# PEER sweep with gates in 2 KB rows, activations in pairs, and gathered slots at 32, 16 and 80

## The reference

```
q = (x @ w_q).reshape(T, 8, 2, 128); s = q . sub_keys      # 128 keys a side, 8 heads
top 16 per side, 16 best of the 256 sums per head -> idx (T, 128); g = softmax(best scores)
a = x . u_tab[idx];  wgt = g * gelu(a)
y = sum over the 128 chosen experts of wgt * v_tab[idx]
```

## Time and profile before

| what | value |
|---|---|
| median of 3 runs | 2556.61 us (2554.44 to 2559.3) |
| profiled execution | 2554.05 us, its span 2552.2 us |
| granted TensorE clock, mean | 0.962 of full speed |
| PE busy | 2294.7 us, 90% |
| DVE / ACT / POOL busy | 68% / 36% / 43% |
| moved by DMA | 771.11 MB, mean 302 GB/s |

### The profile page before, as it was taken

The page is one execution under the profiler, slowest core; times in us unless marked ns, Lnnn a source line. Parts: engine busy times, 40 slices in busy tenths (PEclk is TensorE's granted clock), DMA queues, the critical chain, the costliest instruction groups (busy, mean ns, idle before and its releaser), DMA issues.

```text
span 2552.2 us, 39867 instructions
## 1 busy us (share of the span) xinstructions
PE 2294.7 (90%) x11829; PEld 1696.5 (66%) x11829; DVE 1744.0 (68%) x3945; ACT 912.5 (36%) x1694; POOL 1109.0 (43%) x612
## 2 busy tenths in 40 slices
PE   6697999999877999999989689999998769999998
PEld 3676999999874333333368389989998754444443
DVE  7986798888554766666669856988886553444444
ACT  3254455666542111111044254656665420000001
POOL 2623587777782222222224035777777841111110
PEclk8898999999998999999999799999999989999999
DMA  7423378999999999999942023679999999999995
GB/s 298 157 78 128 110 228 300 383 387 383 403 418 393 387 394 394 394 394 394 378 155 92 0 83 109 185 269 376 383 377 392 420 378 368 369 384 385 374 381 206
DMA packets 284091, 771.11 MB, mean 302 GB/s; under 512 B 26080, under 2 KB 160352, under 8 KB 248544
## 3 DMA queue, kind: packets, MB, share of 16 engines
q1 hardware_dynamic: 169664, 401.76, 44.0%
q0 software_dynamic: 36864, 268.45, 25.9%
q10 hardware_dynamic: 77472, 99.78, 10.8%
HBM read 701.08 MB, written 68.81 MB: 302 GB/s over the span
## 4 chain that ended last, share of the span: by engine, by line
PE 56%; DMA 16%; issue 13%; DVE 8%; POOL 3%; SPq 2%; ACT 2%; ACTq 0%; DVEq 0%; POOLq 0%
PE ps L1718 26%; DMA raw<-in_v 7%; PE ps L1484 7%; PE ps L1485 7%; PE ps L1486 7%; PE ps L1700 4%; POOL w_lo L585 3%; DMA work<-in_uv,picked 2%; DMA hf<-in_uv,picked 2%; DMA hots<-in_uv,picked 1%; DMA uv_stat<-in_uv,picked 1%; SPq L554 1%; DVE ps L1364 1%; DVE ga L1030 1%; PE ps L1653 1%
## 5 line engine op out<-in xcount | busy, mean ns | idle before, releaser
L585 POOL TENSOR_TENSOR w_lo<-raw,w_hi 128x1024 fp32r<-128x1024 f32 x330 | 801.3, 2432 | 573.6 <-ACT w_hi L677 571.5
L1718 PE MATMUL ps<-raw,work 128*128 128x512 f32 x2048 | 906.0, 603 | 68.0 <-DMA raw<-in_v 41.5
L1484 PE MATMUL ps<-h_hi,w_hi 128*128 128x256 f32 (+1 forms) x2560 | 776.4, 303 | 75.2 <-POOL w_lo L585 74.9
L1718 PEld LDWEIGHTS ps<-raw,work 128*128 128x128 f32 x2048 | 392.2, 193 | 580.6 <-issue 576.2
L1485 PE MATMUL ps<-h_lo,w_hi 128*128 128x256 f32 (+1 forms) x2560 | 754.6, 295 | 0.0
L1486 PE MATMUL ps<-h_hi,w_lo 128*128 128x256 f32 (+1 forms) x2560 | 754.3, 295 | 0.0
L1484 PEld LDWEIGHTS ps<-h_hi,w_hi 128*128 128x128 f32 x2560 | 492.3, 192 | 92.6 <-POOL w_lo L585 91.7
L1485 PEld LDWEIGHTS ps<-h_lo,w_hi 128*128 128x128 f32 x2560 | 492.8, 193 | 0.0
L1486 PEld LDWEIGHTS ps<-h_hi,w_lo 128*128 128x128 f32 x2560 | 491.8, 192 | 0.0
L677 ACT ACTIVATE w_hi<-raw 128x1024 fp32r<-128x1024 f32 x330 | 347.7, 1056 | 118.1 <-DMA raw<-in_in 39.0
L1412 DVE TENSOR_TENSOR work<-work 128x256 f32<-128x256 f32 x256 | 106.3, 422 | 412.6 <-DMA work<-g_dram 340.6
(11 more groups left out here) (195 smaller groups left out, 2287.4 us busy)
## 6 DMA issues: line engine op xcount, KB each, us to landing
raw<-in_u SPq DMA_DIRECT2D x256, 512.0 KB, 6.9
raw<-in_v SPq DMA_DIRECT2D x256, 512.0 KB, 8.8
a_dram<-ga ACTq DMA_DIRECT2D x256, 128.0 KB, 7.8
work<-g_dram SPq DMA_DIRECT2D x64, 512.0 KB, 11.3
work<-a_dram ACTq DMA_DIRECT2D x248, 128.0 KB, 9.0
g_dram<-work ACTq DMA_DIRECT2D x16, 1920.0 KB, 11.5
work<-in_mod_w SPq DMA_DIRECT2D x56, 512.0 KB, 10.9
hots<-in_mod_w SPq DMA_DIRECT2D x32, 512.0 KB, 3.6
```

What stands on the lines that cost most here:

```text
L585: nc.gpsimd.tensor_tensor(w_lo[:, m % RING, :], raw[:, m % RING, :], w_hi[:, m % RING, :].bitcast(F32), ALU.subtract).then_inc(lo_ready, 1)
L1484: mm(out, w_hi[:, s, cols], h_hi[:, k, first:], start=n == 0, stop=False)
L1718: last = mm(ps[:, Y_DENSE[NT - ND_TILES + t] + half, :], wf[:, b, t * P:(t + 1) * P], raw[:, s, half * 512:(half + 1) * 512], start=first, ...
```

## The change

Gates are loaded for 16 keys at a time (SPAN), 2 MB in four pieces of 512 KB with rows of 2 KB, after blocks 1, 4, 7 and 10 of a span, for the next span. One buffer lies where `stage` was, the other in `w_hi`, which the sweep doesn't use. The first span's pieces and eight activations are loaded by SP among the last 16 u loads. Activations are stored in pairs (256 KB, rows of 2 KB) after each second block, from two pair buffers, and loaded in pairs, eight blocks ahead. A chunk of gates is stored in one part. Slots are 32 in the table, 16 in the tail (one per two blocks), 80 in the sweep (five per eight blocks). The sweep's bodies on SP and VectorE become turns of 32 blocks; the memset of `a_pad` moves from block 8 to block 24 of the last turn, and the modulation groups keep their blocks.

The diff, without changed counts of semaphores and the bodies that it removes:

```diff
@@ -84,8 +84,12 @@
...
 UBLOCKS = N_KEYS - GBLOCKS - TAIL
-QUAD = 4
-HEAD = 2 * QUAD * CHUNK
+SPAN = 16
+PIECE_AT = (1, 4, 7, 10)
+PIECES = len(PIECE_AT)
+A_PAIRS = 4
+TURN = 2 * SPAN
+TURNS = N_KEYS // TURN
 HOTS = 2
...
@@ -93,10 +97,14 @@
...
 TABLE_STEPS = GBLOCKS // 2
-SWEEP_STEPS = N_KEYS // 2
+SLOT_AT = (0, 2, 4, 5, 7)
+PER_EIGHT = len(SLOT_AT)
+SWEEP_STEPS = N_KEYS // 8 * PER_EIGHT
+TAIL_STEPS = SLOTS - TABLE_STEPS - SWEEP_STEPS
+TAIL_EVERY = TAIL // TAIL_STEPS
 STAIR = (4, 16)
 STAIRS = STAIR[0] * TOPK + (TOPK - STAIR[0]) * STAIR[0]
-assert TABLE_STEPS + TAIL + SWEEP_STEPS == SLOTS
+assert TAIL_STEPS * TAIL_EVERY == TAIL and PER_EIGHT * (TURN // 8) % UVBUFS == 0
 WBUFS = 4
@@ -248,6 +256,7 @@
...
         c_all = keys[:, :, :].rearrange("p a k -> p (a k)").rearrange("p (g d) -> p g d", g=2)
+        a_out = ga[:, :, :].rearrange("p a t -> p (a t)")[:, 0:4 * ND].rearrange("p (a t) -> p a t", a=4)
         unread = ga[:, :, :].rearrange("p a t -> p (a t)")[:, 0:D].bitcast(BF16).rearrange("p (g d) -> p g d", g=2)
...
@@ -313,10 +322,11 @@
...
         after_cols = place[0]
-        g_in = region(2, NCHUNK, QUAD * CHUNK, at=after_cols)
+        a_in = region(2 * A_PAIRS, ND, at=after_cols)
         wf = region(WBUFS, ND)
         uv_work = region(2 * D)
-        a_in = region(4, ND, at=2 * N_KEYS * CHUNK)
+        g_in = (region(NCHUNK, SPAN * CHUNK, at=0),
+                w_hi[:, :, :].rearrange("p r d -> p (r d)").bitcast(F32).rearrange("p (c x) -> p c x", c=NCHUNK))
...
@@ -412,9 +421,9 @@
...
-        a_dram = nc.dram_tensor("a_dram", (N_KEYS, P, ND), F32).ap()
+        a_dram = nc.dram_tensor("a_dram", (N_KEYS // 2, P, 2 * ND), F32).ap()
         g_dram = nc.dram_tensor("g_dram", (NCHUNK, P, N_KEYS * CHUNK), F32).ap()
-        g_quads = g_dram.rearrange("c p (q i t) -> p q c (i t)", i=QUAD, t=CHUNK)
+        g_spans = g_dram.rearrange("c p (q i t) -> p q c (i t)", i=SPAN, t=CHUNK)
...
@@ -464,6 +473,12 @@
...
+            def gates(i, span, n):
+                rows = slice(n * NCHUNK // PIECES, (n + 1) * NCHUNK // PIECES)
+                sp.dma_start(g_in[span % 2][:, rows].unsqueeze(1),
+                             g_spans[:, bass.ds(i * 2 + span, 1), rows]).then_inc(g_loaded[span % 2], 16)
...
@@ -507,58 +522,57 @@
...
                 stream(f"wq{layer}", RING, HS - RING, 4)
-                stream(f"u{layer}", 0, N_KEYS, 4)
+                stream(f"u{layer}", 0, N_KEYS - SPAN, 4)
+                for s in range(2):
+                    sp.wait_ge(g_stored[s], 16 * (layer + 1) * (NCHUNK // 2))
+                    sp.wait_ge(a_stored[s], 16 * (layer * (N_KEYS // 4) + A_PAIRS // 2))
+                for n in range(PIECES):
+                    stream(f"u{layer}", N_KEYS - SPAN + n * (SPAN // PIECES), SPAN // PIECES, SPAN // PIECES)
+                    gates(0, 0, n)
+                    sp.dma_start(a_in[:, 2 * n:2 * n + 2, :].rearrange("p a t -> p (a t)"),
+                                 one(a_dram, n)).then_inc(a_loaded[n], 16)
...
                 stream(name, 0, RING, RING)
-                sp.wait_ge(cols_done, layer + 1)
-                for j in range(4):
-                    sp.wait_ge(a_stored[j], 16 * (layer * (N_KEYS // 4) + 1))
-                    sp.dma_start(a_in[:, j, :], one(a_dram, j)).then_inc(a_loaded[j], 16)
                 for s in range(2):
-                    sp.wait_ge(g_begun[s], 16 * (layer + 1) * (NCHUNK // 2))
-                for s in range(2):
-                    sp.dma_start(g_in[:, s], g_quads[:, s]).then_inc(g_loaded[s], 16)
-                for s in range(2):
-                    sp.wait_ge(g_stored[s], 16 * (layer + 1) * (NCHUNK // 2))
-                for j in range(4):
-                    sp.wait_ge(a_stored[j], 16 * (layer + 1) * (N_KEYS // 4))
+                    sp.wait_ge(a_stored[s], 16 * (layer + 1) * (N_KEYS // 4))
                 if layer == 0:
...
+                def turn(i, final, mods):
+                    for j in range(TURN):
+                        if final and j >= TURN - RING and not after:
+                            return
+                        sp.wait_ge(block_done, i * TURN + (v0 + j + 1))
+                        if not final or j < TURN - RING:
+                            load(name, i * TURN + (j + RING), v0 + j)
+                        else:
+                            load(after, j - (TURN - RING), v0 + j)
+                        span, at = j // SPAN, j % SPAN
+                        if at in PIECE_AT and not (final and span):
+                            gates(i, span + 1, PIECE_AT.index(at))
+                        if j // 8 in mods and j % 2:
+                            sp.wait_ge(mod_summed, i * TURN + (2 * MOD_EARLY - 8 + j + 1))
+                            k = j % 8 // 2
+                            sp.dma_start(mod_late[:, k, :],
+                                         one(io["mod_w"], i * (TURN // 8 * MSLOTS) + (MOD_EARLY + j // 8 * MSLOTS + k))
+                                         ).then_inc(mod_raw[k], 16)
...
+                    turn(0, False, range(1, 4))
+                    with sp.Fori(1, TURNS - 1) as i:
+                        turn(i, False, range(4))
+                    turn(TURNS - 1, True, range(MOD_ROUNDS - 4 * (TURNS - 1)))
+                else:
+                    with sp.Fori(0, TURNS - 1) as i:
+                        turn(i, False, ())
+                    turn(TURNS - 1, True, ())
                 if layer == 0:
...
@@ -651,7 +665,7 @@
...
                     low(R0[u] + b, M0[u] + b)
-                    if b >= UBLOCKS + GBLOCKS or b % 2 == 0:
+                    if b % (2 if b < UBLOCKS + GBLOCKS else TAIL_EVERY) == 0:
                         gather(layer, q)
...
@@ -900,10 +914,13 @@
...
                 projected(i, step, m)
-                since(act, a_stored[j], i * (4 * step) + 16 * (layer * N_KEYS // 4 + count // 4))
-                nc.scalar.activation(ga[:, j, 0:ND], ps[:, PROJ + r % 2, 0:ND], ACT.Gelu).then_inc(proj_taken, 1)
-                act.wait_ge(proj_taken, i * step + (r + 1))
-                act.dma_start(one(a_dram, i * step + count), ga[:, j, 0:ND]).then_inc(a_stored[j], 16)
+                pair = count // 2 % 2
+                since(act, a_stored[pair], i * (4 * step) + 16 * (layer * N_KEYS // 4 + count // 4))
+                nc.scalar.activation(a_out[:, j, :], ps[:, PROJ + r % 2, 0:ND], ACT.Gelu).then_inc(proj_taken, 1)
+                if count % 2:
+                    act.wait_ge(proj_taken, i * step + (r + 1))
+                    act.dma_start(one(a_dram, i * (step // 2) + count // 2),
+                                  a_out[:, j - 1:j + 1, :].rearrange("p a t -> p (a t)")).then_inc(a_stored[pair], 16)
...
@@ -933,7 +950,6 @@
...
                         if j % SETS == 0:
-                            since(act, g_begun[s], i * 16 + layer * 16 * (NCHUNK // 2))
                             since(act, g_stored[s], i * 16 + layer * 16 * (NCHUNK // 2))
...
@@ -945,15 +961,14 @@
...
                             act.wait_ge(g_taken, i * (2 * SETS) + (layer * GBLOCKS + j + 1))
-                            flat = stage[:, s].rearrange("p k t -> p (k t)")
-                            chunk = one(g_dram, i * 2 + s)
-                            act.dma_start(chunk[:, 0:HEAD], flat[:, 0:HEAD]).then_inc(g_begun[s], 16)
-                            act.dma_start(chunk[:, HEAD:], flat[:, HEAD:]).then_inc(g_stored[s], 16)
+                            act.dma_start(one(g_dram, i * 2 + s),
+                                          stage[:, s].rearrange("p k t -> p (k t)")).then_inc(g_stored[s], 16)
...
                     plain(0, UBLOCKS + GBLOCKS + j, 1)
-                    weight(0, 0, TABLE_STEPS + j)
+                    if j % TAIL_EVERY == TAIL_EVERY - 1:
+                        weight(0, 0, TABLE_STEPS + j // TAIL_EVERY)
...
@@ -961,15 +976,17 @@
...
                     for j in range(8):
-                        if j < 4 or not last:
+                        if j % 2 and not last:
                             act.wait_ge(w_ready, i * 8 + (layer * N_KEYS + j + 1))
-                            act.dma_start(a_in[:, j % 4, :], one(a_dram, i * 8 + (j + 4))).then_inc(a_loaded[j % 4], 16)
-                        if j % 2 == 0:
-                            weight(i, 4, TABLE_STEPS + TAIL + j // 2)
-                with act.Fori(0, SWEEP_STEPS // 4 - 1) as i:
+                            n = j // 2
+                            act.dma_start(a_in[:, 2 * n:2 * n + 2, :].rearrange("p a t -> p (a t)"),
+                                          one(a_dram, i * A_PAIRS + (n + A_PAIRS))).then_inc(a_loaded[n], 16)
+                        if j in SLOT_AT:
+                            weight(i, PER_EIGHT, TABLE_STEPS + TAIL_STEPS + SLOT_AT.index(j))
+                with act.Fori(0, N_KEYS // 8 - 1) as i:
                     beside(i, False)
-                beside(SWEEP_STEPS // 4 - 1, True)
+                beside(N_KEYS // 8 - 1, True)
...
```

(50 more changed lines are left out.)

## The result

The changed kernel takes **2536.31 us** (median of 4 runs, 2532.95 to 2537.79), the kernel before 2557.06 beside it: a ratio of 0.9921, 95% interval 0.9908 to 0.9934. That is faster, but by 21 us where 50 were forecast. The profiled execution, the longest of the four, took 2537.79 us with a span of 2536.0.

A forecast was written before the change was run, and what follows sets the result against it. TensorE bounds the table and layer 1's sweep, DMA the tails and layer 0's sweep. Profiled 2554.05 less 20 (layer 0) and 30 (layer 1) gives 2504; with 2.6 for the median, 2507 us, range 2486 to 2548.

The forecast's parts named there:

- the other 192.5 MB go at the rate of the sweep ... I take 409: Layer 0 sweep: all bytes but the last 16 blocks' move at 409 GB/s, 471 us of its 526.
- 55.5: End of each sweep: TensorE sets the last 16 blocks, 3.467 us each, 55.5 us.
- a v load lands in 7.8 us with 10.4 allowed, so 2.6 us of room per load: Sweep, SP's queue: gate pieces pass the v loads within this room, listed under what costs nothing.
- the pairs' wait: Tail: gelu waits for the store issued three blocks earlier, not four; taken as 0, bounds 0 and 31 us a layer.
- I am wrong if the DMA goes idle after the first v blocks of layer 0: Start of layer 0's sweep: SP waits for stores there; idle DMA would void bytes over rate; no size given.
- Tail and gap: Last 32 u blocks until the first v matmul: 108 us instead of 149.4 in each layer, tail 101, gap about 7.
- Bytes: DMA traffic: total unchanged, 16.8 MB of gathers per layer move from tail to sweep; sweeps carry 209 and 177 MB.
- Layer 1: Second layer: sweep 455 us against 443.8, whole layer 563 against 593.2, so -30 us.
- A: Both sweeps: 2 KB rows cost as 512 B rows, 392 GB/s, total -12 us, 2545 us; chance 0.08.
- B: Both sweeps: the DMA keeps up at 418 GB/s, layers gain 30 and 38 us, 2488 us; chance 0.15.
- C: Tails: activation pairs landing in 14.2 us stall them, 132 us not 101; 2569 us, layer 0 alone 2538; chance 0.09.
- D: Sweeps: longer SP and VectorE loops stall SP 5 us per return, 15 us in all, 2522 us; chance 0.08.

The follow-up runs named there:

- eight v buffers: Changed kernel with eight v buffers in the sweep, not four, v loaded eight blocks ahead: 2514.34 us, ratio 0.9839 to the kernel before.
- conditioning early: Changed kernel with conditioning vectors and first four modulation loads issued before the last 16 u loads: 2537.23 us; with eight buffers also, 2513.86.

## Why the prediction was wrong in size

**The step that failed: "the other 192.5 MB go at the rate of the sweep ... I take 409".** That number was read from windows with full queues, and it holds for such windows (median 409). The mean was 394. Put that in the same sum: 192.5 / 394 = 489, and 55.5: 544, measured 544.4. Layer 1: 163.5 / 400 = 409, and 55.5: 464, measured 462.7. Other kernels fit as well, each with its own mean rate:

| layer 0 | mean GB/s | 192.5 MB / rate + 55.5 | measured |
|---|---|---|---|
| after | 394 | 544 | 544.4 |
| 512 B rows | 386 | 554 | 554.2 |
| eight v buffers | 406 | 530 | 530.3 |
| eight, 512 B rows | 395 | 543 | 543.6 |

The windows cover most of the sweep, so this is close to dividing bytes by their own rate and isn't four proofs; it shows that the bytes and the 55.5 us at the end were right and only the rate was off. The error was to say what bytes would go at 409 but not who keeps the queues full. The bounds for the rate, 392 and 418, came from stages where someone always did.

**What made the rate fall** was in the working and priced at nothing: "a v load lands in 7.8 us with 10.4 allowed, so 2.6 us of room per load". The 7.8 was read in layer 1 before, without the moved gathers and without modulation weights on SP's queue. Layer 0's sweep before, then after (KB each, median us to landing):

```profile
raw<-in_v SPq DMA_DIRECT2D x124, 512.0 KB, 9.6
```

```profile
raw<-in_v SPq DMA_DIRECT2D x124, 512.0 KB, 10.1
```

So by the same measure, 10.4 us allowed, the room in that layer was 0.8 us before the change, not 2.6, and after it the median is at the limit. The medians hide the rest: between 770 and 1240 us of after, 46 of the 83 v loads whose landing the trace has took over 10.4 us, up to 20, where before 1 of 28 did, up to 10.8. That row should have been carried over as an unknown cost with an upper bound, in the manner of the pairs' wait.

**The last step: "I am wrong if the DMA goes idle after the first v blocks of layer 0".** It named the danger but the wrong place: the start cost nothing that could be measured (conditioning early gained nothing); the dry queues came all through the sweep, behind stops of TensorE.

**Tail and gap** held: 112.3 and 110.8 for 108. The gap is 6.1 us for 7 (753.85 to 759.96), the tail 106.2 for 101 (647.64 to 753.85), its splits 3.4 us apart for 3.1; its DMA ran at a mean of 389 GB/s, where the check in the prediction had 417. **Bytes** held within 1%. **Layer 1** was 8 us off in the sweep; with eight buffers it gives 455.3 for 455. By layer, eight buffers are 12.6 us (layer 0) and 27.6 (layer 1) under before, for 20 and 30 forecast.

**The whole.** The profiled execution took 2537.79, 34 us over 2504. Tails hold 7 of these, the sweeps 18 and 8, the rest 1. Of the 26 in the sweeps, eight v buffers give back 21.5 (14.1 and 7.4). So with that cure the prediction's sum would be off by 9 us, and 2514 stands beside 2507.

**Rivals.** A is refuted by the narrow rows, though its time, 2545, was nearer than the forecast's 2507: a near number for a wrong reason. B had its rate in windows, never as a mean. C is refuted for this change, though its 2538 for layer 0 alone is the nearest of all: gelu waits 0.8 us for stores in layer 0's tail and 1.0 in layer 1's. C had priced a cost for pairs that take over 9.8 us to land. The trace of after has no landing for these stores; with eight v buffers they take 8.3 us in the median in layer 0's tail, and four blocks take 13.7 us in after's tail, not C's 12 to 12.6, which leaves more room. D: 14 packets of instructions and 2 more on a second queue come in layer 0's sweep (3 and 2 before). None of them lies between 816 and 867 us, around the stop shown above. VectorE has two stops, 11.0 us, that the profile puts down to "issue" at line 1047; they end at 857.2 and 1205.8, each 0.1 us after a modulation load has landed (857.1 and 1205.7), so they are late loads too. The long stops of TensorE come every 16 blocks, not once per 32. With eight buffers at most 4 us of layer 0 are left for D. Its price rested on an assumed stall of 5 us that no row showed, and it wasn't tried by itself.

**Open:** how the 17 us of the kernel with gathers in the tail split between wide gate rows, wide activation rows and early first gates. Restoring 512 B rows costs 27 us, more than all of it, so the rest must be negative or the parts don't add; the runs don't tell.

## What to carry to other kernels

Bytes over rate holds only while someone keeps the queues full: before using it, take each load's landing time from the most crowded stretch that it will meet, and compare that with how far ahead it is issued. Where work is moved into a stage, deepen the buffers of that stage's other loads in the same change; here the move alone gave 2 us, the buffers alone 2 us, and both together 24. A move between two stages that are both DMA-bound is worth nothing in itself (layer 0, 0.6 us with eight buffers); only layer 1, whose sweep had been TensorE's, gained (26 us).

## What the runs showed of the hardware

- A queue's share is not its need: with both backlogged (846 to 860 us), gathers took 61% and SP's queue 33% of the engines, while the loads on which TensorE waited stood on the latter.
- A stop of TensorE costs more than its length. With 7.8 us of idle time the granted clock went to 0.50, was still 0.56 at 864 to 866 us, and the matmuls of 861 to 866 show a median of 1061 ns where 592 is usual.
- The width of rows went on counting between 1 and 2 KB, it seems on the store side too, since the stores' landings of 13.6 to 14.9 us carried the chain of a table: 33.5 MB of gates at 512 B instead of 2 KB cost 27 to 28 us, and activations at 1 KB instead of 2 KB 25 us.
- With eight buffers the DMA of this one core averaged 405 GB/s over 360 us on end (860 to 1220).
